# Wider slots for the side stages of a hybrid decoder step, and the weight sums issued by GpSimd

## The chip, the cores and the metric

One NeuronCore of a Trainium2 chip runs the whole program as one launch. The metric is device time in microseconds from the start to the end of an execution, and less is better. PE is TensorE, DVE is VectorE, ACT is ScalarE, POOL is GpSimd and SP is the sync engine, which here only issues DMAs.

## What is computed

One layer of a decoder with two branches, for a prompt of 2048 tokens and for 8 samples of 8 tokens each. Cut to what matters:

```python
xn = _rmsnorm(x, g_pre)
u = xn @ w_in                                    # 2112 tokens x 1024 -> 10256 columns
z = (glr @ w_gla_lr + b_gla_lr)                  # low-rank decay, from 16 columns of u
o_a, s_new = _gla(q, k, v, log_sigmoid(z) / 16, s0)      # gated linear recurrence, in chunks
y_a = (_rmsnorm(o_a) * silu(gg)) @ w_gla_branch
for (win, dil) in ((128, 1), (512, 4), (2048, 16)):      # dilated windows
    prompt: banded attention;  samples: attention over the cached rows and the 8 new ones
y_b = (softmax-weighted sum of the windows * silu(dg)) @ w_dil_branch
merged = sigmoid(ga) * y_a + sigmoid(gb) * y_b
h = x + _rmsnorm(merged @ w_out, g_post)
h = h + (pe @ w_ple_proj) * sigmoid(h @ w_ple_gate)
```

The outputs are h, the recurrence's states, and the windows' caches of keys and values.

## The kernel before

**The frame.** The product x @ w_in fills most of the run. Its 10240 wide columns are 20 column tiles of 512, and the prompt is taken in two phases of 1024 tokens, so there are 40 column tiles in time, each with two halves. A half takes seven products of a seven-product scheme for 2x2 blocks (forms P1, P6, P2, P7, P4, P5, P3 in this order) in place of eight, and each product is three fp16 matmuls (high part by high, low by high, high by low). A column tile has 336 such matmuls (L849, L851); the samples' 48 (L860) come with those of phase 0.

**Slots.** Every engine's program is one loop over 740 numbered slots, 17 for a column tile of phase 0 (8 and 9 for its halves) and 20 for one of phase 1. In each slot an engine issues its part of the product first and then what the side stages have in that slot. The slot's length in time is what PE needs for its matmuls of that slot, and the engines meet through semaphores alone. An engine that is late in a slot makes later ones late in turn.

**The weights of the next column tile.** SP loads 512 columns of w_in into two tiles `raw` (L695). The seven forms need four sums of their quarters, made in place: P7, P6, P4, P5 (`sum`, L714, L718, L722, L725). ACT then casts each form to its high part (`cut_hi`, L703) and DVE makes the low part (`cut_lo`, L707). This is timed by tables in slots from the middle of the column tile before: the high parts at 4 (P1), 5 (P2), 6 (P7), 7 (P6), 9 (P4), 10 (P5) and 11 (P3), the low part one slot later. Before the change DVE makes the sum P7 at 2, and each other sum right behind the low part that sets its quarter free: P6 behind P1, P4 behind P2, P5 behind P7. PE takes P1 at 9 (phase 0), P6 some 1.1 slots later, and so on.

**The side stages that the change touches.**

- Tokens (`Inputs`): the second 1024 prompt tokens are loaded, normed, summed and split (L442, L551), turned by a DMA transpose (L570) and stored in four pairs, the first at slot 16 and each 11 slots after the last.
- Slices (`Cutter`): 30 slices of the later weights (mixer weights) are loaded, cast by ACT (`cut_hi`, L2257), subtracted by DVE (`cut_lo`, L2263) and both parts stored by SP (L2244, L2245), from slot 95, one every 4 slots. ACT's cast waits until both stores of the slice before have landed.
- Recurrence (`Gla`, phase 0): eight steps from slot 72, one every 6 slots. `SampleGla` follows at slot 130.
- Samples (`Samples`): from slot 236, one sample every 15 slots; u is the slot within one. Caches of keys and values are loaded (ACT and POOL issue them), DVE makes row sums in slots u = 1, 3, 5, 7 (L2164, L2168) from rows that POOL loads two steps ahead (L1963), and PE turns those sums at the end of u = 8 (L2088).
- The windows of the prompt begin at slots 409, 481, 547 and the recurrence's phase 1 at 625; the mixer (L2888) follows the loop.

POOL's part before the change: norms and sums of the tokens, DMA issues of the side stages, and copies of the caches (L3070).

## Time and profile before

| what | value |
|---|---|
| median of 3 runs | 2868.7 us (2867.64 to 2869.06) |
| the profiled execution, its own time | 2873.31 us |
| its span | 2871.4 us |
| PE busy | 2671.5 us (93%) |
| DVE busy | 1767.6 us (62%) |
| ACT busy | 1035.5 us (36%) |
| POOL busy | 430.5 us (15%) |
| mean granted clock of PE | 0.971 |

The profile's page gives each engine's busy time and share of the span. A busy PE may run at either of two granted clocks, 2.4 GHz (1.0) or 1.2 GHz (0.5), so time is lost in two ways: as idle time of PE, and as busy time at the lower clock. The product's loop takes about the first 2235 us, the mixer the rest.

### The profile page before, as it was taken

What the parts mean: (1) busy time and instruction counts of PE and PEld (TensorE: products, weight loads), DVE (VectorE), ACT (ScalarE), POOL (GpSimd) and SP (SyncE); (2) the same over time, 40 slices, a digit from 0 to 9 for tenths busy, and PEclk for the clock granted to TensorE, in tenths of its full rate; (3) what the DMA queues carried; (4) which work ended last, traced back from release to release, by engine and by line L of the source; (5) the groups of instructions that cost most, each with busy time, mean ns of one, the idle gap of its engine ahead of it and who ended that gap; (6) DMA issues with size and microseconds to landing.
All of it is one profiled execution on the core that took longest, in us unless ns stands there. A gap on an engine that the chain in (4) does not pass through costs nothing. (4 is left out here: it accounts for less than half of the span.)

```text
span 2871.4 us, 54212 instructions
## 1 busy us (share of the span) xinstructions
PE 2671.5 (93%) x21916; PEld 2041.6 (71%) x21916; DVE 1767.6 (62%) x3181; ACT 1035.5 (36%) x1880; POOL 430.5 (15%) x649
## 2 busy tenths in 40 slices
PE   5788989899989999899999999999999999999998
PEld 4676878678877788788888888888887444444444
DVE  6575766665656656656677666767666455555552
ACT  4233443232222222222334445535423344444441
POOL 5132102210112122101112211011100000000000
PEclk8999999999999999999999999999999999999999
DMA  5698666888777879667757766455546976566552
GB/s 152 153 275 285 229 224 237 312 281 296 262 271 250 258 265 286 233 233 259 264 185 240 232 224 212 139 170 186 186 181 181 313 217 143 158 176 167 163 116 57
DMA packets 370058, 622.39 MB, mean 217 GB/s; under 512 B 199196, under 2 KB 204899, under 8 KB 365330
## 3 DMA queue, kind: packets, MB, share of 16 engines
q1 hardware_dynamic: 311554, 352.11, 39.2%
q0 software_dynamic: 44000, 233.26, 24.8%
q10 hardware_dynamic: 14256, 33.56, 3.3%
q8 instruction: 175, 2.87, 0.4%
q14 instruction: 73, 0.60, 0.1%
HBM read 429.15 MB, written 244.66 MB: 235 GB/s over the span
## 5 line engine op out<-in xcount | busy, mean ns | idle before, releaser
L851 PE MATMUL out<-w_hi,x_hi 128*128 128x256 f16 x3136 | 872.0, 278 | 64.0 <-DVE w_lo L707 24.7
L851 PE MATMUL out<-w_lo,x_hi 128*128 128x256 f16 x3136 | 871.8, 278 | 0.0
L851 PE MATMUL out<-w_hi,x_lo 128*128 128x256 f16 x3136 | 871.1, 278 | 0.0
L773 DVE SCALAR_TENSOR_TENSOR stage<-out,stage 128x512 f32<-128x512 f32 (+1 forms) x567 | 378.7, 680 | 362.4 <-PE out L851 257.9
L851 PEld LDWEIGHTS out<-w_hi,x_hi 128*128 128x128 f16 x3136 | 313.1, 100 | 119.1 <-DVE w_lo L707 27.4
L849 PE MATMUL out<-x_hi,w_hi 128*128 128x256 f16 x1344 | 369.3, 275 | 26.4 <-DVE w_lo L707 20.0
L849 PE MATMUL out<-x_hi,w_lo 128*128 128x256 f16 x1344 | 369.2, 275 | 0.0
L849 PE MATMUL out<-x_lo,w_hi 128*128 128x256 f16 x1344 | 369.1, 275 | 0.0
L703 ACT ACTIVATE w_hi<-raw 128x1024 f16<-128x1024 f32 x280 | 290.6, 1050 | 196.4 <-DVE raw L718 47.8
L707 DVE SCALAR_TENSOR_TENSOR w_lo<-raw,w_hi 128x1024 f16<-128x1024 f32 x280 | 343.9, 1232 | 7.6 <-ACT w_hi L703 7.5
L851 PEld LDWEIGHTS out<-w_hi,x_lo 128*128 128x128 f16 x3136 | 312.8, 100 | 42.8 <-issue 1.3
L851 PEld LDWEIGHTS out<-w_lo,x_hi 128*128 128x128 f16 x3136 | 312.7, 100 | 42.3 <-issue 1.1
L849 PEld LDWEIGHTS out<-x_hi,w_hi 128*128 128x128 f16 x1344 | 132.5, 99 | 47.6 <-DVE w_lo L707 22.2
L761 ACT ACTIVATE stage<-out 128x512 f32<-128x512 f32 (+1 forms) x81 | 47.7, 589 | 291.8 <-PE out L851 205.9
L849 PEld LDWEIGHTS out<-x_lo,w_hi 128*128 128x128 f16 x1344 | 132.6, 99 | 16.3
L1856 DVE CUSTOM_DVE_ANT_0 score<-out,mask 128x128 f32<-128x128 f32 (+1 forms) x192 | 69.8, 363 | 120.7 <-PE out L1802 110.2
L849 PEld LDWEIGHTS out<-x_hi,w_lo 128*128 128x128 f16 x1344 | 132.5, 99 | 16.0
L1841 ACT ACTIVATE prob<-score,result 128x128 f32<-128x128 f32 (+1 forms) x192 | 87.4, 455 | 103.5 <-DVE result L1859 103.0
L1831 ACT ACTIVATE query<-qT 128x128 f32<-128x128 f32 x128 | 54.8, 428 | 184.9 <-PE out L1791 184.9
L2888 PE MATMUL out<-mix_w_hi,mix_zTh 128*128 128x512 f16 (+1 forms) x408 | 118.8, 379 | 0.8 <-DMA mix_zTl<-mix_z_rowl 0.8
L2888 PE MATMUL out<-mix_w_lo,mix_zTh 128*128 128x512 f16 (+1 forms) x408 | 118.8, 379 | 0.0
L2888 PE MATMUL out<-mix_w_hi,mix_zTl 128*128 128x512 f16 (+1 forms) x408 | 118.8, 379 | 0.0
(354 smaller groups left out, 4279.3 us busy)
## 6 DMA issues: line engine op xcount, KB each, us to landing
raw<-in_w_in SPq DMA_DIRECT2D x80, 1024.0 KB, 8.9
out<-in_cache_kv_w POOLq DMA_DIRECT2D x64, 1020.0 KB, 9.0
U<-stage SPq DMA_DIRECT2D x224, 256.0 KB, 5.8
UT<-stage SPq DMA_DIRECT2D x96, 256.0 KB, 6.9
sw_kc<-in_cache_kv_w ACTq DMA_DIRECT2D x24, 1024.0 KB, 11.0
sw_vc<-in_cache_kv_w POOLq DMA_DIRECT2D x24, 1024.0 KB, 9.6
sw_rows<-U POOLq DMA_DIRECT2D x32, 512.0 KB, 7.6
out<-in_cache_kv_w POOLq DMA_DIRECT2D x16, 1008.0 KB, 7.5
```

What stands on the lines that cost most here:

```text
L703: act.activation(self.w[0][f][:, :, :], self.sources[f], ACT.Copy, scale=W_SCALE).then_inc(self.hi_ready, 1)
L707: dve.scalar_tensor_tensor(out=self.w[1][f][:, :, :], in0=self.sources[f], scalar=W_SCALE, in1=self.w[0][f][:, :, :], op0=ALU.mult, op1=AL ...
L761: act.activation(self.spot(D, 1, 0, us), self.shaped(D, self.product(D, P1, us), us), ACT.Copy, scale=1.0 / W_SCALE).then_inc(self.act_kep ...
L773: return dve.scalar_tensor_tensor(out=out, in0=self.shaped(D, self.product(D, f, us), us), scalar=1.0 / W_SCALE, in1=other, op0=ALU.mult, ...
L849: return pe.matmul(out.rearrange("p (a t) -> p a t", t=P), w[:, k, d * P:(d + 1) * P], x[:, 2 * u:2 * u + 2, f * HALF_K + k, :], start=sta ...
L851: return pe.matmul(out, x[:, 2 * d + u, f * HALF_K + k, :], w[:, k, :], start=start, stop=stop)
L1831: act.activation(self.query[n % 2][:, :], self.queries(h, b, dil), ACT.Copy)
L1841: act.activation(self.prob[n % 2][:, a:, :], self.score[n % 2][:, a:, :], ACT.Exp, scale=SCALE, bias=result[:, b, HD:HD + 1], accum_out=re ...
L1856: dve.tensor_tensor_reduce(self.score[n % 2][:, a:, :], self.SCORE[:, a * P:2 * P].rearrange("p (a j) -> p a j", j=P), self.mask[:, a:, :] ...
L2888: made = pe.matmul(made, x, w, start=(k == 0 and i == 0), stop=(k == last and i == 2))
```

## The change

It moves six tables and two kinds of work, and what is computed stays the same.

- The four sums of a column tile's weights are issued on POOL (in slots 1, 5, 7 and 8 counted from the middle of the column tile before). Those of the first column tile stay on DVE.
- Tokens: pairs begin at slot 18 and every 15 slots, and their loads are at slots 7, 8, 13 and 27, as soon as buffers are free, in place of 4 slots ahead of each pair.
- Recurrence, phase 0: from slot 84 every 8 slots; `SampleGla` at 163.
- Slices: from slot 100 every 5 slots; the high part is stored one slot after its cast and the low part one slot after that, each with its own semaphore, so that ACT waits for the high part's store alone and DVE for the low part's.
- Samples: from slot 264 every 17 slots.
- Some semaphores are reused (`left`, `later`), which makes room for the new ones.

```diff
-SUM_AT = 2
+SUM_AT = {P7: 1, P6: 5, P4: 7, P5: 8}
...
-GLA_SLOTS, GLA_PERIODS = (GLA_TILES * TILE_PARTS[0] + 4, 625), (6, 7)
-GLA_SAMPLE_SLOT = 130
-SAMPLE_SLOT, SAMPLE_PERIOD = 236, 15
+GLA_SLOTS, GLA_PERIODS = (84, 625), (8, 7)
+GLA_SAMPLE_SLOT = 163
+SAMPLE_SLOT, SAMPLE_PERIOD = 264, 17
...
-CUT_SLOT, CUT_PERIOD = 95, 4
+CUT_SLOT = 100
+CUT_TIMES = [5 * i for i in range(30)]
...
-    FIRST_SLOT, EVERY = 16, 11
+    FIRST_SLOT, EVERY = 18, 15
+    LOAD_SLOTS = (7, 8, 13, 27)
...
-            if slot == self.base(k) - 4:
+            if slot == self.LOAD_SLOTS[k - self.SAMPLE - 1]:
...
                     self.cut_lo(dve, H, f)
-                    if f in NEXT_SUM:
-                        self.sum(dve, H, NEXT_SUM[f])
-            if at == SUM_AT:
-                self.sum(dve, H, P7)
...
+    def pool(self, pool, q):
+        for H, _, at in self.coming(q):
+            for f in (P7, P6, P4, P5):
+                if at == SUM_AT[f]:
+                    self.sum(pool, H, f)
...
+        i = self.at(r - 1)
+        if i is not None:
+            sp.wait_ge(self.hi_cut, i + 1)
+            sp.dma_start(self.cut_hi[:, i, :], self.hi[:, :]).then_inc(self.hi_stored, 16)
         i = self.at(r - 2)
         if i is not None:
             sp.wait_ge(self.lo_cut, i + 1)
-            sp.dma_start(self.cut_hi[:, i, :], self.hi[:, :]).then_inc(self.stored, 16)
-            sp.dma_start(self.cut_lo[:, i, :], self.lo[:, :]).then_inc(self.stored, 16)
+            sp.dma_start(self.cut_lo[:, i, :], self.lo[:, :]).then_inc(self.lo_stored, 16)
...
-            wait(act, self.stored, 32 * i)
+            wait(act, self.hi_stored, 16 * i)
+            wait(act, self.lo_cut, i)
...
             dve.wait_ge(self.hi_cut, i + 1)
+            wait(dve, self.lo_stored, 16 * i)
...
                 G, d, c = place(q)
+                projection.pool(pool, q)
                 inputs.pool(pool, q)
```

On DVE, in the fourth sample (u = 4 to 7), where the low parts of P1, P2, P7 and P6 of the next column tile stand among the sample's row sums. Before the change (L707 is a low part, L718, L722 and L725 the sums P6, P4 and P5, L2164 and L2168 the row sums, L773 takes a product over):

```order
L707 SCALAR_TENSOR_TENSOR w_lo<-raw,w_hi 128x1024
L718 TENSOR_TENSOR raw<-raw 128x4x256
L773 SCALAR_TENSOR_TENSOR stage<-out,stage 128x2x256
L707 SCALAR_TENSOR_TENSOR w_lo<-raw,w_hi 128x1024
L722 TENSOR_TENSOR raw<-raw 128x4x256
L2164 TENSOR_TENSOR sw_rows<-sw_kc,sw_rows 128x1024
L2168 TENSOR_REDUCE sw_sT<-sw_rows 128x2x4
L773 SCALAR_TENSOR_TENSOR stage<-out,stage 128x2x256 x2
L707 SCALAR_TENSOR_TENSOR w_lo<-raw,w_hi 128x1024
L725 TENSOR_TENSOR raw<-raw 128x4x256
L773 SCALAR_TENSOR_TENSOR stage<-out,stage 128x2x256
L707 SCALAR_TENSOR_TENSOR w_lo<-raw,w_hi 128x1024
```

In the changed kernel the same place of DVE (its lines stand a few further down: L709 is the low part, L775 the product taken over, L2171 and L2175 the row sums) reads:

```order
L709 SCALAR_TENSOR_TENSOR w_lo<-raw,w_hi 128x1024
L775 SCALAR_TENSOR_TENSOR stage<-out,stage 128x2x256
L709 SCALAR_TENSOR_TENSOR w_lo<-raw,w_hi 128x1024
L2171 TENSOR_TENSOR sw_rows<-sw_kc,sw_rows 128x1024
L2175 TENSOR_REDUCE sw_sT<-sw_rows 128x2x4
L775 SCALAR_TENSOR_TENSOR stage<-out,stage 128x2x256 x2
L709 SCALAR_TENSOR_TENSOR w_lo<-raw,w_hi 128x1024
L775 SCALAR_TENSOR_TENSOR stage<-out,stage 128x2x256
L709 SCALAR_TENSOR_TENSOR w_lo<-raw,w_hi 128x1024
L2171 TENSOR_TENSOR sw_rows<-sw_kc,sw_rows 128x1024
```

The three sums are gone from among the low parts, and the rest stands in the same order.

On POOL, one whole sample of phase 0 in the changed kernel (L716, L720, L724 and L727 are the sums P7, P6, P4 and P5, L1970 the load of rows, L1955, L1976 and L1996 loads of the queries, keys and values):

```order
L716 TENSOR_TENSOR raw<-raw 128x4x256
L1970 DMA sw_rows<-U 128x2x512
L1955 DMA sw_new_k<-U 8x512
L1955 DMA sw_new_v<-U 8x512
L1955 DMA sw_q<-U 8x512
L720 TENSOR_TENSOR raw<-raw 128x4x256
L1970 DMA sw_rows<-U 128x2x512
L1976 DMA sw_new_k<-U 8x512 x3
L724 TENSOR_TENSOR raw<-raw 128x4x256
L1970 DMA sw_rows<-U 128x2x512
L727 TENSOR_TENSOR raw<-raw 128x4x256
L1970 DMA sw_rows<-U 128x2x512
```

Before, POOL had the loads alone here; now three of a sample's four loads of rows stand right behind a sum.

On SP, two slices late in the slices' stage (CUT_HI and CUT_LO are the stores of the two parts, `cut_raw` the load of a later slice, U and UT the product's results). Before the change:

```order
L2244 DMA CUT_HI<-cut_hi 128x1024
L2245 DMA CUT_LO<-cut_lo 128x1024
L2240 DMA cut_raw<-in_w_out 128x1024
L904 DMA U<-stage 128x512 x4
L2244 DMA CUT_HI<-cut_hi 128x1024
L2245 DMA CUT_LO<-cut_lo 128x1024
```

In the changed kernel:

```order
L2251 DMA CUT_HI<-cut_hi 128x1024
L908 DMA UT<-stage 128x512
L2255 DMA CUT_LO<-cut_lo 128x1024
L908 DMA UT<-stage 128x512
L2247 DMA cut_raw<-in_w_out 128x1024
L2251 DMA CUT_HI<-cut_hi 128x1024
```

The store of the high part has left the store of the low part and goes a slot earlier.

## Rows read from the trace of the kernel before

**Rows 1.** The page: span and busy time of PE and PEld, DVE, ACT, POOL.

```profile
span 2871.4 us, 54212 instructions
PE 2671.5 (93%) x21916; PEld 2041.6 (71%) x21916; DVE 1767.6 (62%) x3181; ACT 1035.5 (36%) x1880; POOL 430.5 (15%) x649
```

**Rows 2.** Stretches: length, busy (instructions) of PE, PEld, DVE, ACT, POOL, clock, DMA, GB/s.

```profile
110.00:330.00 220.00, 190.73 (x1738) 160.80 (x1737) 149.65 (x174) 73.97 (x98) 54.76 (x56) 0.94 0.80 247
330.00:586.00 256.00, 232.38 (x2052) 192.75 (x2050) 162.36 (x251) 103.72 (x143) 48.42 (x77) 0.95 0.74 257
586.00:765.00 179.00, 165.96 (x1545) 144.57 (x1544) 108.08 (x119) 49.86 (x56) 8.16 (x18) 0.96 0.81 282
765.00:1212.00 447.00, 409.65 (x4785) 352.61 (x4784) 277.92 (x387) 99.35 (x143) 99.97 (x171) 0.96 0.79 263
1212.00:1909.00 697.00, 680.99 (x5844) 600.29 (x5843) 473.95 (x1290) 272.80 (x763) 101.92 (x148) 1.00 0.64 215
1909.00:2235.00 326.00, 305.33 (x2539) 257.98 (x2538) 214.60 (x337) 128.00 (x180) 24.45 (x34) 0.97 0.57 191
```

**Rows 3.** The stretch right behind a long gap of PE, same columns.

```profile
172.00:176.50 4.50, 4.50 (x23) 3.19 (x22) 0.86 (x1) 0.00 (x0) 0.00 (x0) 0.50 1.59 201
```

**Rows 4.** Timeline, PE: start, us, engine, line, instruction [idle before, what ended it].

```profile
171.78 0.40 PE L849 MATMUL out<-x_hi,w_hi 128*128 128x256 f16 x1 [8.76 <-DVE w_lo L707]
223.54 0.39 PE L851 MATMUL out<-w_hi,x_hi 128*128 128x256 f16 x1 [8.30 <-DVE w_lo L707]
```

**Rows 5.** Timeline: DVE at a late load, and PE behind two of them.

```profile
259.54 1.23 DVE L714 TENSOR_TENSOR raw<-raw 128x1024 f32<-128x1024 f32 x1 [12.06 <-DMA raw<-in_w_in]
...
261.42 0.28 PE L851 MATMUL out<-w_hi,x_hi 128*128 128x256 f16 x1 [3.97 <-DVE stage L773]
...
805.61 0.40 PE L851 MATMUL out<-w_hi,x_hi 128*128 128x256 f16 x1 [5.50 <-DVE stage L773]
```

**Rows 6.** Slices: ACT's idle time before L2257 (us, times), the stores' landing, timeline.

```profile
  DMA CUT_LO<-cut_lo: 155.8, 23
...
DMA to landing us min/median/max: 2.3/6.1/14.1
...
420.90 1.15 ACT L2257 ACTIVATE cut_hi<-cut_raw,cut_gains 128x1024 f16<-128x1024 f32 x1 [12.01 <-DMA CUT_LO<-cut_lo]
...
422.68 0.37 PE L1236 MATMUL out<-prompt_lowrank,prompt_decay_w 51*128 51x128 f16 x2 [4.38 <-ACT prompt_k_endT L1284]
...
535.88 0.79 PE L1547 MATMUL out<-sample_v,sample_att 128*128 128x256 f32 x1 [4.28 <-ACT sample_o L1588]
```

**Rows 7.** Timeline, PE: the longest gap in the recurrence of phase 0.

```profile
393.50 0.77 PE L1261 MATMUL out<-prompt_v,prompt_k_endT 128*128 128x256 f32 x1 [4.81 <-DVE prompt_att L1330]
```

**Rows 8.** The fourth sample: DVE's first and last row of 15, PE; PE's waits there.

```profile
975.33 0.69 DVE L773 SCALAR_TENSOR_TENSOR stage<-out,stage 128x512 f32<-128x512 f32 x1 [0.42 <-PE out L851]
...
990.29 1.22 DVE L2168 TENSOR_REDUCE sw_sT<-sw_rows 128x8 f32<-128x1024 f32 x1
...
991.57 0.47 PE L2088 MATMUL out<-identity,sw_sT 128*128 128x128 f32 x1 [6.12 <-DVE sw_sT L2168]
...
PE out L2088 <- DVE sw_sT L2168: 25.6, 6, 7.2
```

**Rows 9.** Lines: ns min/median/max of DVE's sum, low part and POOL's token sum; one collision.

```profile
L714 DVE TENSOR_TENSOR raw<-raw x40: 1212/1216/1812, 13.4 to 2168.3; 128x1024 f32<-128x1024 f32 x40
...
L707 DVE SCALAR_TENSOR_TENSOR w_lo<-raw,w_hi x280: 1203/1215/2279, 15.1 to 2188.2; 128x1024 f16<-128x1024 f32 x140
...
L456 POOL TENSOR_TENSOR sums<-x x7: 1268/1278/2177, 10.4 to 224.8; 128x512 f32<-128x512 f32 x7
...
14.21 2.12 POOL L461 TENSOR_TENSOR sums<-x,sums 128x512 f32<-128x512 f32 x1
...
15.14 2.28 DVE L707 SCALAR_TENSOR_TENSOR w_lo<-raw,w_hi 128x1024 f16<-128x1024 f32 x1
```

**Rows 10.** The rows' load L1963: us from issue to landing.

```profile
DMA to landing us min/median/max: 5.3/7.6/17.3
```

More of the change, by code:

```diff
@@ L1060, in queue, with left @@
                 sp.dma_start(self.L[:, SEQ:TOKENS], self.last[:, :]).then_inc(self.stored, 16)
+    def left(self):
+        return [(self.cut, 3 * PHASES), (self.made, PHASES), (self.kept, 2 * self.CHUNKS + 3)]
     def done(self, eng, phase):
@@ L1917, in __init__ @@
         self.rows_loaded = [one(f"rows_loaded{s}") for s in range(self.RING)]
-        self.k_loaded = [one(f"k_loaded{p}") for p in range(len(self.K_PIECES) + 1)]
+        self.k_loaded = [later(f"sw_k_loaded{p}") for p in range(len(self.K_PIECES))] + [Later(one("new_k_loaded"), 0)]
         self.v_loaded = one("v_loaded")
@@ L1973, in load_k @@
             after(q, self.k_turned, c * N_TURNED)
-            self.load_new(q, c, self.new_k, U_DK, self.k_loaded[p])
+            self.load_new(q, c, self.new_k, U_DK, self.k_loaded[p].sem)
             return
@@ L1982, in load_k @@
             after(q, self.k_turned, (c - 1) * N_TURNED + blocks.stop)
-        q.dma_start(self.kc[:, blocks, :], src).then_inc(self.k_loaded[p], 16)
+        q.dma_start(self.kc[:, blocks, :], src).then_inc(self.k_loaded[p].sem, 16)
     def load_v(self, q, c):
@@ L2058, in tensor @@
             p = self.turned_piece(n)
-            pe.wait_ge(self.k_loaded[p], 16 * (c + 1) * (1 if n < N_CACHE else GROUPS))
+            after(pe, self.k_loaded[p], 16 * (c + 1) * (1 if n < N_CACHE else GROUPS))
             after(pe, self.k_kept, c * N_TURNED + i - 1)
@@ L2161, in vector @@
             p = max(p for p, (g, low, _) in enumerate(self.K_PIECES) if CACHE_BLOCKS.index((g, low)) <= first)
-            dve.wait_ge(self.k_loaded[p], 16 * (c + 1))
+            after(dve, self.k_loaded[p], 16 * (c + 1))
             dve.wait_ge(self.rows_loaded[x % self.RING], 16 * (x // self.RING + 1))
@@ L2224, in __init__ @@
         self.lo_cut = one("lo_cut")
-        self.stored = one("stored")
+        self.hi_stored = one("hi_stored")
+        self.lo_stored = one("lo_stored")
     def at(self, r):
-        i, u = divmod(r, CUT_PERIOD)
-        return i if u == 0 and 0 <= i < len(self.slices) else None
+        return CUT_TIMES.index(r) if r in CUT_TIMES else None
     def gain(self, i):
@@ L2235, in queue @@
     def queue(self, sp, r):
-        i = self.at(r + CUT_PERIOD + 1)
+        i = self.at(r + 5)
         if i is not None:
@@ L2243, in queue @@
             sp.wait_ge(self.lo_cut, i + 1)
-            sp.dma_start(self.cut_hi[:, i, :], self.hi[:, :]).then_inc(self.stored, 16)
-            sp.dma_start(self.cut_lo[:, i, :], self.lo[:, :]).then_inc(self.stored, 16)
+            sp.dma_start(self.cut_lo[:, i, :], self.lo[:, :]).then_inc(self.lo_stored, 16)
     def done(self, eng):
-        wait(eng, self.stored, 32 * len(self.slices))
+        wait(eng, self.hi_stored, 16 * len(self.slices))
+        wait(eng, self.lo_stored, 16 * len(self.slices))
     def scalar(self, act, r):
@@ L2961, in run_layer @@
                 windows = Windows((core.bind(part)[0], sem), side, U, UT, a["window_mask"], identity, OG, kv_prompt[0])
-        left = iter(inputs.left() + sample_gla.left() + prompt_gla.left() + windows.left())
+        left = iter(inputs.left() + sample_gla.left() + prompt_gla.left() + windows.left() + lowrank.left())
         def later(name):
@@ L3032, in _ @@
                     lowrank.queue(sp, phase, q - LOWRANK_SLOTS[phase])
-                if q == CUT_SLOT - CUT_PERIOD - 4:
+                if q == CUT_SLOT - 8:
                     lowrank.done(sp, 0)
```

## The prediction, made before the changed kernel ran

> **What bounds the kernel now.** I read the page first: PE is busy 2671.5 of 2871.4 us [rows 1], so at most 200 us of idle time, and what PE does at the lower clock, can be won. The view of stretches says where that lies. From 110 to 1212 us (phase 0, with tokens, recurrence, slices and samples beside the product) PE lacks 29.3, 23.6, 13.0 and 37.4 us (length less busy time) and its clock stands at 0.94 to 0.96; from 1212 to 1909 us (windows) it lacks 16.0 us at a clock of 1.00, and from 1909 to 2235 us 20.7 us at 0.97 [rows 2]. A gap costs more than its length: right behind the one that ends at 171.78 us the granted clock is 0.50, which is 1.2 GHz, for 4.5 us [rows 3]. PE was busy all that time and did half the work, so 2.25 us are lost besides the gap; I charge that to each gap over 3.5 us. The change touches phase 0 above all, so I then went through PE's gaps there and asked of each what ended it.
>
> **Tokens (110 to 330 us).** Two gaps of 8.76 and 8.30 us end on the low part of a weight [rows 4]. Counting off 336 product matmuls a column tile, both stand 24 matmuls into one, at P6, in slots 35 and 52. DVE was behind: the low parts of the seven forms must be made in slots 13 to 20 of a column tile's 17 (up to P6 in 13 to 16), and pairs 2 and 4, with bases 27 and 49, put their splitting in slots 31 and 32 and their scaling in 49 and 50, into just these. A third gap, 3.97 us, has another cause: DVE itself had stood 12.06 us at the sum P7, whose load was late, and took no products over meanwhile [rows 5]. With bases 18, 33, 48 and 63 the splitting of the second pair is at 37 and 38 and out of the way, loads are early, and a late load now stops POOL and not DVE. Removed: 8.76 + 8.30 + 3.97 + 3 x 2.25 = 27.8 us. But pairs 3 and 4 now scale in slots 48, 49, 63 and 64, beside the low parts, with POOL's token sums (four of 1.28 us each [rows 9]) among the weight sums. I put back 10 us for that. **Net -18 us** (-28 to -5).
>
> **Slices (345 to 765 us).** ACT waits 155.8 us, in 23 of 30 slices, for the store of the low part; a store takes 6.1 us to land in the median, at most 14.1 [rows 6]. Before, two slots (some 5 to 6 us) lie between the issue of the stores and the next cast. While ACT stands it makes no high parts and takes nothing else over: the wait of 12.01 us that ends at 420.90 us delays `prompt_k_endT`, and PE stands 4.38 us for it; the gap of 4.28 us at 535.88 us ends on ACT too [rows 6]. After the change four slots lie between each store and its waiter, 10 to 13 us, over the median and a little under the worst. From 586 to 765 us little else runs than slices, so all its loss counts: 13.0 us idle, and of the clock's deficit of 0.04 x 179 = 7.2 us some six tenths, 4.3 us (part of the lower clock falls into gaps and costs nothing). That makes 17.3 us, and 2 x (4.3 + 2.25) = 13.1 us with the two gaps ahead of it: 30 us. Since P6's chain stays tight (below), I take three quarters. **-23 us** (-30 to -10).
>
> **Recurrence (300 to 500 us).** What else the stretch 330 to 586 us lost is 23.6 + 0.6 x 12.8 - 13.1 = 18 us; its longest gap is 4.81 us behind DVE's `prompt_att` [rows 7]. Eight slots a step in place of six thin DVE's work per slot by a quarter, but the masked copy and the product behind it stay one slot apart. I take half. **-9 us** (-16 to 0).
>
> **Weight sums from DVE to POOL.** DVE loses 39 x 4 instructions of 1.22 us [rows 9], 190 us in all, and none of that is a gain by itself, as PE is not waiting for DVE's mean. What counts is DVE in the four slots in which it makes P1, P2, P7 and P6. The price on POOL: its tensor_tensor on 128x512 takes 1.28 us alone, so 2.5 us for a sum of 128x1024 (an estimate from that row). And the two engines block each other: L707, whose inputs both lie in SBUF, took 2.28 us in place of 1.22 beside a POOL sum, which itself took 2.12 in place of 1.27 [rows 9]. So a sum of 2.5 us on POOL may hold DVE's next low part for up to 2.3 us, against 1.22 us saved.
>
> The Trainium skill says the same as a rule (SBUF — State Buffer, section SBUF: two separate sides): the port pair that DVE and GpSimd share is an exclusive lock held for a whole instruction, and a DVE instruction with two SBUF inputs takes part in it. By that rule alone the offload is worth about nothing wherever DVE is behind; had the two not blocked each other, each column tile would have 4.9 us less of DVE. The collision in rows 9 agrees.
>
> The samples show what that does. In the fourth one DVE works without a pause from 975.33 to 991.51 us, 16.2 us for 15 instructions, and PE has stood 6.12 us [rows 8]. Without three sums of 1.22 us that is 12.5 us and a gap of 2.5 us; with POOL holding DVE by 1 to 1.8 us at each of three low parts it is 6 us again. This sample began 9 slots into a column tile. A period of 17 and a start at 264 = 15 x 17 + 9 give all five samples that lie in phase 0 this place, while the eight of now lose 25.6 us, in six gaps [rows 8], and 6 x 2.25 us of clock, 39 us in all. Five at 6.1 + 2.25 are 42 us: no change; at 2.5 + 2.25, -15; and if the rows that POOL loads behind a sum come late (7.6 us to landing, up to 17.3 [rows 10], used three slots later), up to +15. The 5.50 us at 805.61 us, again behind a late load of weights [rows 5], go, as the caches' first loads start six slots ahead of the weights and no longer just with them: -7. **Samples together -7 us** (-22 to +8).
>
> In the windows PE lacks only 16.0 of 697 us [rows 2]. ACT must wait longer for a sum of 2.5 us, and DVE is held now and then: **+5 us** (0 to +20) for 13 column tiles. In the recurrence's phase 1, whose slots don't move, both effects meet: **0** (-8 to +8).
>
> **Costed at nothing.** SP issues as many DMAs as before; POOL's waits for stores and for DVE's results name work of two slots earlier, so they don't hold a sum that stands behind them. POOL's busy time grows by 39 x 4 x 2.5 = 390 us to some 820 of 2871: not a bound.
>
> **The sum.** -18 - 23 - 9 - 7 + 5 + 0 = -52 us. From the profiled execution's 2873.3 us that gives 2821; the median of the runs lies 4.6 us below that execution, so **2817 us**. Its own range is 2798 to 2842, from the terms' ranges taken together and not all at one end.
>
> **The rivals.**
>
> *DVE is freed for real.* If POOL's sums mostly fall where DVE takes products over (from PSUM, which no row shows blocked), the samples win 15 more, the put-back at the tokens is 4 and not 10, and phase 1 gains its 8: 2817 - 29 = 2788. For it: DVE waits for PE often enough outside phase 0's crowded slots. Against: the sums stand right behind low parts, where DVE goes on to the next one. Chance 0.19.
>
> *Gaps move and don't go.* P6's chain (low part of P1, sum, cast, low part) is no shorter, so the slots in which slices and tokens were late turn out late by P6 again: tokens and slices bring a third. -14 - 5 - 7 + 5 = -21: about 2848. Chance 0.14 for that; 0.06 that it lies within 0.2% of now (2863 to 2874).
>
> *POOL makes P6 late, and the kernel slower.* The place is P6 in each of the 19 column tiles from 110 to 1156 us. On POOL the sum waits for a low part (1.2 us), takes 2.5 in place of 1.22, the low part of P6 waits behind the next sum (up to 2.5), and three sums (3.7) no longer stand ahead of it: +1.3 us; with three DMA issues between the sums, +3. PE takes P6 only 5 slots behind the low part of P1, some 13 to 16 us. At 2.5 us and 2.25 of clock each, 19 x 4.75 = 90 us against the 52 won: 2817 + 90 = 2907. It decides from 2.7 us a tile with the clock. Against it: the low parts saved from ahead of P6 nearly pay for it. Chance 0.13. It is also what the rule of the Trainium skill (same page and section) would make of it, if POOL got the lock first each time.
>
> That the change doesn't do what it says is out: on DVE the sums are gone and on POOL they stand.
>
> **How the numbers follow.** The forecast itself has 0.48 of the chance. All cases but the last two are faster: 0.48 + 0.19 + 0.14 = 0.81; same 0.06; slower 0.13. A measurement can tell about 0.2%, 6 us, from no change. The range takes the forecast, most of the better case, and the lesser gain up to no change: 2785 to 2872.
>
> **What would show it.** Tokens: no gaps of over 4 us in the first 330 us behind the first column tile. Slices: ACT's wait for CUT_LO gone, for CUT_HI under 30 us. Sums: POOL's rows at 2.5 us alone and 3.5 or more beside DVE, L709's longest at 3 us or more. Samples: five gaps at the turning of the row sums, each 2 to 7 us; if they are gone, the lock bites less than I think. I am wrong if PE shows a gap at P6 in most column tiles (slower), or if PE's idle time in phase 0 behind the first column tile, 103 us now (110 to 1212 us), stays over 75 us (tokens and slices were not the cause).

## The result: 0.6% slower, and the profile after

The changed kernel takes 2885.9 us in the median (2883.2 to 2889.3) against 2868.9 us before: a ratio of 1.0058 (95% interval 1.0039 to 1.0078). The forecast was 2817 us, with a range of 2785 to 2872; the time lies outside it and on the other side of no change. The profiled execution took 2889.3 us, its span is 2887.4.

The page after, span and busy time, answers to [rows 1]:

```profile
span 2887.4 us, 54244 instructions
PE 2666.2 (92%) x21916; PEld 2041.8 (71%) x21916; DVE 1734.1 (60%) x3025; ACT 1036.0 (36%) x1880; POOL 824.9 (29%) x805
```

POOL is at 825 us, as forecast (some 820). DVE lost 156 sums of 1.22 us, 190 us, and is only 33.5 us less busy. Where most of that went stands in the costliest groups of after (busy us, mean ns | idle before, and what ended it):

```profile
L709 DVE SCALAR_TENSOR_TENSOR w_lo<-raw,w_hi 128x1024 f16<-128x1024 f32 x280 | 455.5, 1632 | 14.5 <-ACT w_hi L705 14.3
...
L720 POOL TENSOR_TENSOR raw<-raw 128x1024 f32<-128x1024 f32 x39 | 99.8, 2560 | 442.2 <-DVE w_lo L709 442.2
```

The low parts (L709, L707 before) are the same 280 instructions. Their mean was 1232 ns before and is 1632 ns now: 112 us more of DVE. The next largest are the recurrence's `prompt_to_end` (8.0 us more) and the samples' `sw_rows` (5.7). And POOL stands 442 us ahead of P6's sum (L720), waiting for a low part of DVE: whatever POOL has queued behind that sum waits as well.

By stretches (columns as in [rows 2]); the bounds are the ends of the same column tiles, so that the same products stand in a row of before and of after; matmuls of the side stages have moved between rows (1738 and 1627 PE instructions in the first). First after, then, of before, the stretch with the samples, which [rows 2] cuts elsewhere:

```profile
107.50:311.30 203.80, 174.66 (x1627) 147.33 (x1625) 131.43 (x118) 58.77 (x75) 96.92 (x70) 0.96 0.87 238
311.30:552.10 240.80, 224.59 (x1982) 193.52 (x1982) 162.94 (x230) 109.53 (x147) 63.41 (x57) 0.96 0.68 239
552.10:754.00 201.90, 185.45 (x1723) 154.18 (x1721) 118.91 (x140) 56.88 (x72) 76.35 (x76) 0.95 0.81 282
754.00:1299.80 545.80, 489.76 (x5459) 421.41 (x5457) 315.19 (x405) 122.05 (x167) 203.78 (x221) 0.95 0.77 257
1299.80:1922.50 622.70, 604.49 (x5174) 536.30 (x5172) 407.60 (x1196) 255.63 (x744) 196.66 (x178) 0.99 0.64 213
1922.50:2251.50 329.00, 302.94 (x2539) 256.99 (x2538) 217.75 (x313) 128.34 (x181) 89.28 (x61) 0.97 0.57 190
```

```profile
764.50:1286.10 521.60, 483.41 (x5458) 418.25 (x5456) 321.90 (x437) 116.09 (x161) 103.96 (x179) 0.96 0.77 258
```

Length less PE's busy time, before and after: tokens 29.3 and 29.1 us; recurrence 23.6 and 16.2; slices 13.0 and 16.5; samples 38.2 and 56.0. Together 104 and 118 us. At 754 us the changed kernel is still 10 us ahead (764.5 before), although part of the recurrence's work has moved into the slices' column tiles. The samples' column tiles take that away and 14 us more (1299.8 against 1286.1); the windows are even, and the recurrence's phase 1 loses 3 us.

What PE waits for after (us in all, times, longest):

```profile
PE out L2095 <- DVE sw_sT L2175: 49.3, 8, 6.9
PE out L855 <- DVE w_lo L709: 34.5, 10, 6.7
PE out L853 <- DVE w_lo L709: 15.6, 4, 5.8
```

The turning of a sample's row sums (L2095; L2088 before) cost 25.6 us in six gaps [rows 8] and costs 49.3 in eight. The two gaps of 8.76 and 8.30 us at P6 [rows 4] are gone, but fourteen others stand at P6 with 50 us (18 with 44.7 us before, those two among them). Three more stalls are new or larger (PE's timeline): in the recurrence, at P6, and in the windows.

```profile
310.73 0.39 PE L1243 MATMUL out<-prompt_lowrank,prompt_decay_w 51*128 51x128 f16 x2 [6.09 <-DMA prompt_decay_w<-WS]
...
496.47 0.39 PE L855 MATMUL out<-w_hi,x_hi 128*128 128x256 f16 x1 [6.65 <-DVE w_lo L709]
...
1538.51 0.48 PE L1798 MATMUL out<-identity,k 128*128 128x128 f32 x1 [8.74 <-ACT kT L1839]
```

The first of them comes from a load that POOL issued late, behind the sum P7 (L716) whose own weights came late:

```profile
298.52 2.35 POOL L716 TENSOR_TENSOR raw<-raw 128x1024 f32<-128x1024 f32 x1 [26.14 <-DMA raw<-in_w_in]
...
302.38 0.54 POOL L1204 DMA_DIRECT2D prompt_decay_w<-WS  x1
```

"A late load now stops POOL and not DVE", which the prediction counted as a gain, has this price: what POOL issues next stops too.

ACT's wait for the slices' stores, 155.8 us in 23 [rows 6], is now for the high part alone:

```profile
ACT cut_hi L2269 <- DMA CUT_HI<-cut_hi: 62.2, 7, 16.3
```

### The profile page after: what moved, and what is told of

Read it like the earlier page. It is cut to its first block and busy times, and to the rows that moved or that the text cites. A ratio compares the mean times of both kernels' runs of the same rounds, so it can differ in the third digit from the quotient of the medians.

```text
span 2887.4 us, 54244 instructions
## 1 busy us (share of the span) xinstructions
PE 2666.2 (92%) x21916; PEld 2041.8 (71%) x21916; DVE 1734.1 (60%) x3025; ACT 1036.0 (36%) x1880; POOL 824.9 (29%) x805
## 5 line engine op out<-in xcount | busy, mean ns | idle before, releaser
L775 DVE SCALAR_TENSOR_TENSOR stage<-out,stage 128x512 f32<-128x512 f32 (+1 forms) x567 | 378.4, 680 | 451.6 <-PE out L855 317.8
L709 DVE SCALAR_TENSOR_TENSOR w_lo<-raw,w_hi 128x1024 f16<-128x1024 f32 x280 | 455.5, 1632 | 14.5 <-ACT w_hi L705 14.3
L720 POOL TENSOR_TENSOR raw<-raw 128x1024 f32<-128x1024 f32 x39 | 99.8, 2560 | 442.2 <-DVE w_lo L709 442.2
L716 POOL TENSOR_TENSOR raw<-raw 128x1024 f32<-128x1024 f32 x39 | 96.0, 2461 | 241.3 <-DMA raw<-in_w_in 241.0
L853 PEld LDWEIGHTS out<-x_lo,w_hi 128*128 128x128 f16 x1344 | 134.0, 100 | 17.8 <-issue 0.2
## 6 DMA issues: line engine op xcount, KB each, us to landing
U<-stage SPq DMA_DIRECT2D x224, 256.0 KB, 4.4
UT<-stage SPq DMA_DIRECT2D x96, 256.0 KB, 5.7
sw_vc<-in_cache_kv_w POOLq DMA_DIRECT2D x24, 1024.0 KB, 10.6
```

The lines of the kernel that those rows point to most:

```text
L709: dve.scalar_tensor_tensor(out=self.w[1][f][:, :, :], in0=self.sources[f], scalar=W_SCALE, in1=self.w[0][f][:, :, :], op0=ALU.mult, op1=AL ...
L716: eng.tensor_tensor(self.sources[P7], self.sources[P7], self.sources[P3], ALU.subtract).then_inc(self.sum_ready, 1)
L720: eng.tensor_tensor(self.sources[P6], self.sources[P1], self.sources[P7], ALU.subtract).then_inc(self.sum_ready, 1)
L775: return dve.scalar_tensor_tensor(out=out, in0=self.shaped(D, self.product(D, f, us), us), scalar=1.0 / W_SCALE, in1=other, op0=ALU.mult, ...
L853: return pe.matmul(out.rearrange("p (a t) -> p a t", t=P), w[:, k, d * P:(d + 1) * P], x[:, 2 * u:2 * u + 2, f * HALF_K + k, :], start=sta ...
```

## Experiments

Medians are compared with that of the kernel before in the same comparison (2868.6 to 2871.4 us).

**1. The sums, with the new spacing and with the old.** In one kernel the sums go back to VectorE; in the other they alone are moved.

```diff
--- after
+++ sums_on_vector
-SUM_AT = {P7: 1, P6: 5, P4: 7, P5: 8}
+SUM_AT = 2
...
                     self.cut_lo(dve, H, f)
+                    if f in NEXT_SUM:
+                        self.sum(dve, H, NEXT_SUM[f])
+            if at == SUM_AT:
+                self.sum(dve, H, P7)
...
-                projection.pool(pool, q)
```

> The changed kernel with its weight sums put back on VectorE, in their old places; all wider spacing stays. Theory A (the sums on GpSimd cost what the spacing wins: VectorE's low parts are held, P6 comes late, loads stand behind sums in POOL's queue): the fourteen gaps at P6 (49 us together) and the stall of 6.09 us at 310.73 us go or fall to half, the eight gaps at the turning of the samples' sums fall from 5.9 to some 2.5 us, so 2800 to 2835 us. Rival B (the samples' new spacing costs it, whoever makes the sums): 2870 to 2890 us, with the eight gaps still at 5 to 7 us. The prediction's own terms without its term for the sums would give about 2820 us.

> The kernel before with only the weight sums moved to GpSimd. Theory A: slower than before by 30 to 60 us, 2900 to 2930 us, with gaps at P6 in many column tiles. Rival B (sums harmless, the spacing costs): within 6 us of before, 2863 to 2875 us. The prediction priced this part at 0 to +20 us.

Measured: 2872.7 us with all the spacing and the sums on VectorE (1.0022 of before, 1.0002 to 1.0041); 2874.6 us with the sums moved alone (1.0022, 1.0005 to 1.0038). Both times lie in rival B's range and outside theory A's. But the sums do cost, 13 us with the new spacing and 6 with the old, and **all the spacing together gains nothing without them**. With the sums back, the turnings still cost 45.8 us in eight gaps. Neither theory holds alone.

**2. The samples' place.** Moved alone in the kernel before; then at another place in the changed kernel, and there with the sums on VectorE too (both_vector_273).

```diff
--- before
+++ samples_alone
-SAMPLE_SLOT, SAMPLE_PERIOD = 236, 15
+SAMPLE_SLOT, SAMPLE_PERIOD = 264, 17
--- after
+++ samples_273
-SAMPLE_SLOT, SAMPLE_PERIOD = 264, 17
+SAMPLE_SLOT, SAMPLE_PERIOD = 273, 16
```

> The kernel before with the samples alone moved, to slot 264 and every 17. The prediction's term is -7 us (-22 to +8): 2847 to 2877, most likely 2862 us. Theory D: five turnings at P6's slots with 6 us each and three in the short slots of phase 1, where the rows land late, in place of 25.6 us in all: 2880 to 2896 us, with eight gaps at the turning of 45 us or more together.

> The changed kernel with the samples at slot 273 and every 16 slots in place of 264 and 17; sums stay on GpSimd. The turning of the row sums then stands outside the slots in which VectorE makes P1, P2, P7 and P6, in all samples but one or two. Theory A: the gaps at the turning shrink only where no sum of POOL holds VectorE or a load; 2865 to 2880 us. Rival B: the eight gaps fall from 49 us to under 20, with their clock 2840 to 2855 us.

> Both of the above: all spacing of the changed kernel, sums on VectorE, samples at slot 273 and every 16. Theory A: a few us below the kernel with the sums back alone, 2790 to 2825 us. Rival B: 2835 to 2855 us, the same as with the samples moved alone.

Measured: 2890.4 us alone (1.0066, 1.0039 to 1.0093), **19 us slower**, as theory D said; 2886.2 us with 273 and the sums on GpSimd, no change; 2858.6 us with 273 and the sums on VectorE (0.9976, 0.9949 to 1.0002; ten runs from 2848 to 2886), 14 us below the kernel with 264. Neither theory's range held at 273. So the place costs, but at 273 four samples turn in phase 1, and their gaps stay (39.2 and 32.3 us in all eight; of the 32.3, with the sums on VectorE, the four in phase 0 have 0.2 to 2.5 us each and the four in phase 1 3.7 to 9.8). PE's waits at the turning, samples_alone:

```profile
PE out L2088 <- DVE sw_sT L2168: 45.2, 8, 6.7
```

The eight gaps have two causes. Five samples start nine slots into a column tile, and their last step meets the low parts of P2, P7 and P6. In after DVE has no pause there, and PE waits 5.9 us for the last row below (timeline, DVE):

```profile
946.90 1.22 DVE L709 SCALAR_TENSOR_TENSOR w_lo<-raw,w_hi 128x1024 f16<-128x1024 f32 x1
948.03 0.68 DVE L775 SCALAR_TENSOR_TENSOR stage<-out,stage 128x512 f32<-128x512 f32 x1
948.63 2.99 DVE L709 SCALAR_TENSOR_TENSOR w_lo<-raw,w_hi 128x1024 f16<-128x1024 f32 x1
951.54 1.21 DVE L2171 TENSOR_TENSOR sw_rows<-sw_kc,sw_rows 128x1024 f32<-128x1024 f32 x1
952.79 1.22 DVE L2175 TENSOR_REDUCE sw_sT<-sw_rows 128x8 f32<-128x1024 f32 x1
```

Here 2.99 in place of 1.22 us is a sum of POOL (948.21 to 950.54 us). With the sums on VectorE the gap is 6.11 us: what the offload saves, the wait gives back. The other three samples lie in phase 1, where a column tile is cut into 20 slots and not 17, and a slot without other work is 37.3 / 20 = 1.9 us (two column tiles of phase 1 took 74.5 us before). DVE there waits for the rows themselves (after, DVE and then POOL):

```profile
1225.95 1.23 DVE L2171 TENSOR_TENSOR sw_rows<-sw_kc,sw_rows 128x1024 f32<-128x1024 f32 x1 [6.17 <-DMA sw_rows<-U]
...
1216.35 0.75 POOL L1970 DMA_DIRECT2D sw_rows<-U  x1 [6.01 <-DVE sw_sT L2175]
```

The load can be issued only when the step two before it has freed its buffer, and lands some 9 us later, in slots of 1.9 us. Without any sum on POOL it is the same (4.57 us for these rows). In the kernel before, one sample of eight turned in phase 1, which begins at 1156 us, and had the longest gap (before, PE):

```profile
1187.53 0.47 PE L2088 MATMUL out<-identity,sw_sT 128*128 128x128 f32 x1 [7.25 <-DVE sw_sT L2168]
```

**3. The tokens and POOL's copies.** In the kernel with all the spacing and the sums on VectorE, SP's transposition of the second pair took 32.96 us; the eight transpositions of these pairs before took 4 to 10. POOL issues four of the copies that shift the caches within 6 us, the last two just then (timeline, SP and POOL); copies_apart moves these two from slot 44 to slot 231:

```profile
175.71 1.11 POOL L3081 DMA_DIRECT2D out<-in_cache_kv_w  x2
180.27 32.96 SPq L572 DMA_TRANSPOSE row1h<-row0h  x1
180.72 0.96 POOL L3081 DMA_DIRECT2D out<-in_cache_kv_w  x2 [3.90 <-PE out L851]
```

```diff
--- sums_on_vector
+++ copies_apart
-SHIFT_PAIRS = (range(3, 27), range(42, 62))
+SHIFT_PAIRS = ((3, 4, *range(6, 28)), range(42, 62))
```

> The kernel with all the new spacing and the sums on VectorE, but without the two cache copies that POOL issues in slot 44; they are issued at slot 231. Theory C: with the new spacing SP's transposition of the second pair of token tiles begins beside these copies and takes 33 to 41 us where it took 4 to 8, and everything behind it on SP comes late; apart, it takes under 11 us and the stall of 11 us in the tokens goes: 2855 to 2862 us, against 2872.7 with the copies there. Rival: the transposition is slow for another reason, or its delay is hidden: 2867 to 2876 us.

Measured: 2859.8 us (0.9959, 0.9946 to 0.9972), 13 us less. The transposition now:

```profile
179.89 6.90 SPq L572 DMA_TRANSPOSE row1h<-row0h  x1
```

In that kernel column tiles 1 to 4 lose 17.8 us of PE, against 33.4 with the copies there and 29.3 before. The fair comparison is recurrence_alone (below), where the recurrence has left these column tiles too and the tokens are as before: 26.2 us. So the wider tokens do gain, some 8 us, once nothing stands in SP's way. In after the second transposition of this pair took 22.4 us and the first landed 29 us after its issue.

**4. Slices and recurrence**, each alone on the kernel before; the slices keep their period of four.

```diff
--- before
+++ stores_apart
+        i = self.at(r - 1)
+        if i is not None:
+            sp.wait_ge(self.hi_cut, i + 1)
+            sp.dma_start(self.cut_hi[:, i, :], self.hi[:, :]).then_inc(self.hi_stored, 16)
         i = self.at(r - 2)
         if i is not None:
             sp.wait_ge(self.lo_cut, i + 1)
-            sp.dma_start(self.cut_hi[:, i, :], self.hi[:, :]).then_inc(self.stored, 16)
-            sp.dma_start(self.cut_lo[:, i, :], self.lo[:, :]).then_inc(self.stored, 16)
+            sp.dma_start(self.cut_lo[:, i, :], self.lo[:, :]).then_inc(self.lo_stored, 16)
...
-            wait(act, self.stored, 32 * i)
+            wait(act, self.hi_stored, 16 * i)
+            wait(act, self.lo_cut, i)
...
+            wait(dve, self.lo_stored, 16 * i)
--- before
+++ recurrence_alone
-GLA_SLOTS, GLA_PERIODS = (GLA_TILES * TILE_PARTS[0] + 4, 625), (6, 7)
-GLA_SAMPLE_SLOT = 130
+GLA_SLOTS, GLA_PERIODS = (84, 625), (8, 7)
+GLA_SAMPLE_SLOT = 163
```

> The kernel before with one part alone: the stores of a slice's high and low part are issued and waited for apart; period and all other places as before. The prediction's term for slices was -23 us with the period of five. If that is right, three slots in place of two between a store and its waiter bring most of it: 2848 to 2858 us, with ACT's wait for stores under 80 us. Rival (what the slices lose, VectorE's chain to P6 loses anyway): 2864 to 2872 us.

> The kernel before with the recurrence alone moved: every 8 slots from 84, samples' recurrence from 163. The prediction's term is -9 us (0 to -16): 2856 to 2866 us. Theory E: no gain, 2868 to 2878 us, with gaps at P6 in the recurrence's column tiles and the slices, now beside the samples' recurrence, no better.

Measured: stores apart 2852.5 us (0.9941, 0.9924 to 0.9958), **17 us faster**, though ACT still waits 106.8 us; recurrence alone 2871.4 us (1.0012, 0.9998 to 1.0026), no gain. Eight slots a step put two steps into 16 of a column tile's 17 slots, so every second one meets P6 again, with gaps of 5.06 and 5.42 us at slots 120 and 137 (4.42 and 0.47 us before). More is lost behind it: column tiles 9 to 12 lack 24.7 us of PE, against 13.0 before. `SampleGla` now begins in them, beside the slices; a slice's store, which there took 20.2 us to land, holds up ACT, and ACT holds up PE (recurrence_alone, ACT and then PE):

```profile
595.84 1.06 ACT L2257 ACTIVATE cut_hi<-cut_raw 128x1024 f16<-128x1024 f32 x1 [21.96 <-DMA CUT_LO<-cut_lo]
...
597.44 0.39 PE L851 MATMUL out<-w_hi,x_hi 128*128 128x256 f16 x1 [9.00 <-ACT stage L761]
```

The stores apart gain mostly in the recurrence's column tiles: the stretches of 256.0 and 179.0 us [rows 2] take 239.1 and 175.0.

**5. What the parts are worth together.** Tokens wide with the copies apart, stores apart with the old period, sums on VectorE; the samples at 236 or 227; then the recurrence every 6 slots again. Beside these, stores_samples is stores_apart with the samples at 227 and every 15, and nothing else moved.

```diff
--- copies_apart
+++ spaced_236
-CUT_SLOT = 100
-CUT_TIMES = [5 * i for i in range(30)]
+CUT_SLOT = 95
+CUT_TIMES = [4 * i for i in range(30)]
-SAMPLE_SLOT, SAMPLE_PERIOD = 264, 17
+SAMPLE_SLOT, SAMPLE_PERIOD = 236, 15
--- spaced_236
+++ spaced_227
-SAMPLE_SLOT, SAMPLE_PERIOD = 236, 15
+SAMPLE_SLOT, SAMPLE_PERIOD = 227, 15
--- spaced_227
+++ spaced_recur6
-GLA_SLOTS, GLA_PERIODS = (84, 625), (8, 7)
-GLA_SAMPLE_SLOT = 163
+GLA_SLOTS, GLA_PERIODS = (84, 625), (6, 7)
+GLA_SAMPLE_SLOT = 142
```

> Tokens and recurrence as in the changed kernel, with copies and transposition apart; slices with stores apart but at the old start and period (95, 4); samples at their old places (236, 15); sums on VectorE. Theory D (the samples' new place is what costs the spacing its gain, since three of them now turn in phase 1, whose slots of 1.9 us are too short for a load of rows of 6 to 16 us): 2830 to 2850 us. Rival (the samples' place matters little): 2855 to 2865 us, as with the copies apart.

> The same with the samples at slot 227 and every 15, so that seven of the eight turn in phase 0 and the last at its very end. Theory D: 6 to 14 us less than with 236, 2820 to 2840 us, and no gap over 4 us at a turning. Rival: the same time as with 236 within 5 us.

> The kernel before with two parts: a slice's stores apart (old period), and the samples at slot 227 and every 15. Tokens, recurrence and sums as before. Theory D: the samples give here too what they gave between 236 and 227 with all spaced, 12 us, or a little more: 2834 to 2842 us against 2852.5 with the stores alone. Rival (the gain of 227 hangs on the spacing of the rest): 2848 to 2855 us.

> The kernel with tokens spaced, copies and transposition apart, slices 95 and 4, samples 227 and 15, sums on VectorE, and now the recurrence every 6 slots from 84 (samples' recurrence at 142) in place of every 8 from 84 (163). Theory E: eight slots a step gain nothing, since two steps in 16 of a column tile's 17 slots fall on P6 in nearly the same place tile after tile (gaps of 5.06 and 5.43 us at slots 120 and 137): 2825 to 2838 us against 2843.3. Rival, the prediction's (six slots a step are too thin for VectorE): 2848 to 2856 us.

Measured: 2854.8, 2843.3, 2833.5 and **2824.5 us** (the last 0.9849 of before, 0.9825 to 0.9872). With 236 I was wrong: no gain over the stores alone, since the later recurrence took back what the tokens gave (column tiles 1 to 4, which it has left in part, take 193 us in place of 219 in stores_apart; 9 to 12, into which its end has moved, 203 in place of 175). From 236 to 227 the samples gain 12 us, on the old spacing 19 (2852.5 to 2833.5). The turnings are the lesser part of that (27.4 to 24.8 us and 29.2 to 24.1, with gaps over 4 us left where I expected none); a gap behind late weights in column tile 13, of 6.04 and 6.84 us, goes as well. Six slots a step, with `SampleGla` at 142, gain 19 us over eight: column tiles 5 to 8 lack 17.2 us of PE in both kernels, 9 to 12 lack 6.4 in place of 19.8.

**6. Why the sums cost.** On stores_samples (2833.5 us) all sums go to GpSimd as in the change (stores_samples_pool); then they stand behind the loads of the same slot; then only P4 and P5 go, in the place that the change gives them.

```diff
--- stores_samples_pool
+++ loads_first
-                projection.pool(pool, q)
                 inputs.pool(pool, q)
...
                 side_queue(pool, q)
+                projection.pool(pool, q)
--- stores_samples
+++ sums_half
+POOL_AT = {P4: 7, P5: 8}
...
-                    if f in NEXT_SUM:
+                    if f == P1:
                         self.sum(dve, H, NEXT_SUM[f])
...
+    def pool(self, pool, q):
+        for H, _, at in self.coming(q):
+            for f in (P4, P5):
+                if at == POOL_AT[f]:
+                    self.sum(pool, H, f)
```

> The same with the weight sums on GpSimd: the price of the sums where little else is late. Theory A: 10 to 20 us more than with the sums on VectorE, 2846 to 2860 us, with L709-like low parts of over 1.5 us in the mean and new gaps at P6 and behind POOL's loads. Rival (the sums cost only where they meet the samples' bad place): within 4 us of the same kernel with sums on VectorE.

> The kernel with a slice's stores apart, samples at 227 and sums on GpSimd (2859.7 us; 2833.5 with sums on VectorE), with POOL's sums issued behind the loads and stores of the same slot, not ahead of them. Theory F (the sums cost because they wait for VectorE's low parts and hold the loads queued behind them): the stall of 8.64 us in the windows goes, 2840 to 2850 us. Rival G (the price is the lock and the longer way to P6): 2855 to 2866 us, the stall in the windows gone or not, the gaps at P6 as they were.

> The same kernel with P7 and P6 summed on VectorE and only P4 and P5 on GpSimd. Rival G, way to P6: the gaps at P6 are those of the kernel with all sums on VectorE, and so is the time within 6 us, 2830 to 2840 us. Rival G, lock alone: about half of the price of 26 us stays, 2843 to 2850 us. Theory F, queue: sums of P4 and P5 wait for VectorE too, and hold the loads: 2843 us or more, with the stall in the windows there.

Measured: 2859.7, 2854.9 and 2845.7 us. The sums cost **26 us** where less else is late, more than I expected. Against stores_samples, the stretches of tokens, slices, samples and the recurrence's phase 1 are 8, 4, 8 and 10 us longer, that of the windows 3 us shorter. The queue (theory F) is a part: with the sums in front, POOL waits 15 us for a low part and issues the windows' loads behind it. (In the order that POOL has for one sample of the changed kernel, all four loads of rows stand right behind a sum, and not three.) In after, timeline of POOL ahead of the stall at 1538.51 us:

```profile
1516.71 2.35 POOL L720 TENSOR_TENSOR raw<-raw 128x1024 f32<-128x1024 f32 x1 [15.31 <-DVE w_lo L709]
1519.02 1.58 POOL L1729 DMA_DIRECT2D k<-U  x2
```

Behind the loads the stall is gone and the windows' stretch is 10.6 us shorter (618.9 to 608.3), but the samples lose 7 of it, the tokens 5, and the time falls by 5 only. Half of the sums cost half, 12 us, and the gaps at P6 stay although P7 and P6 are summed on VectorE, while the stall in the windows that theory F wanted is absent. All gaps at P6 are 44.9 us in stores_samples, 59.3 with all sums on POOL, 60.6 with the loads first and 60.6 with half. The same P6 in stores_samples, with all sums on POOL, and with half (timeline, PE):

```profile
576.02 0.28 PE L851 MATMUL out<-w_hi,x_hi 128*128 128x256 f16 x1 [2.22 <-DVE w_lo L707]
```

```profile
584.68 0.39 PE L853 MATMUL out<-w_hi,x_hi 128*128 128x256 f16 x1 [4.08 <-DVE w_lo L707]
```

```profile
584.14 0.28 PE L856 MATMUL out<-w_hi,x_hi 128*128 128x256 f16 x1 [3.66 <-DVE w_lo L708]
```

So it is not P6's longer way, and the queue is a lesser part. That the rest is the lock between the two engines is argued from the durations; no run takes the lock alone away. In after 115 low parts meet a sum of POOL (of weights or tokens) and take 2.2 us in the mean, the other 165 take 1.22. The Trainium skill (SBUF — State Buffer, section SBUF: two separate sides) makes the shared port pair an exclusive lock and counts in a VectorE instruction with two SBUF inputs. The trace agrees: L709 and L2171 are held (five of L2171 meet a sum and take 2.4 us in the mean, the others 1.21), while L775, with one input in PSUM, took 0.68 us in the mean in its 155 cases beside a sum (128x512), 0.69 without.

**7. The sums in the windows alone.** In the windows the sums behind the loads had given the shortest stretch; so they are moved there alone, on the fastest kernel.

```diff
--- spaced_recur6
+++ windows_on_pool
+POOL_TILES, POOL_AT = range(23, 34), {P7: 1, P6: 5, P4: 7, P5: 8}
...
-                    if f in NEXT_SUM:
+                    if f in NEXT_SUM and H not in POOL_TILES:
...
+    def pool(self, pool, q):
+        for H, _, at in self.coming(q):
+            for f in (P7, P6, P4, P5):
+                if at == POOL_AT[f] and H in POOL_TILES:
+                    self.sum(pool, H, f)
...
                 side_queue(pool, q)
+                projection.pool(pool, q)
```

> The fastest kernel so far (spaced_recur6, 2824.5 us) with the weight sums of column tiles 23 to 33 alone, the windows, on GpSimd, and there behind the loads of the same slot. Theory H (the sums on GpSimd cost where VectorE is crowded and gain in the windows, where it is not: the stretch of column tiles 23 to 33 took 608.3 us with POOL's sums behind the loads, 621.9 with sums on VectorE): 2808 to 2816 us. Rival G (the lock costs everywhere, and the shorter stretch came from elsewhere): 2822 to 2832 us.

Measured: **2810.8 us** (0.9806, 0.9783 to 0.9829), 13.6 us less. The stretch of the windows without and with it (columns as in [rows 2]):

```profile
1239.00:1861.10 622.10, 607.38 (x5175) 534.84 (x5173) 430.06 (x1240) 256.01 (x745) 98.06 (x140) 1.00 0.63 214
```

```profile
1238.00:1847.10 609.10, 601.06 (x5174) 534.58 (x5173) 410.73 (x1197) 257.74 (x746) 195.87 (x182) 1.00 0.65 219
```

PE lacks 8.0 us in place of 14.7 and is itself busy for 6.3 us less with the same products; why its busy time falls no run here tells. With the sums on POOL the low parts are held there as elsewhere, 31 of 77 meeting a sum (DVE by lines in these stretches, without and then with):

```profile
L709 DVE SCALAR_TENSOR_TENSOR w_lo<-raw,w_hi 128x1024 f16<-128x1024 f32 x77 | 93.4, 1215 | 0.0
```

```profile
L710 DVE SCALAR_TENSOR_TENSOR w_lo<-raw,w_hi 128x1024 f16<-128x1024 f32 x77 | 123.5, 1605 | 0.0
```

So it is not because the low parts are spared that the sums pay there. In the windows some six tenths of VectorE's instruction time go to instructions that read PSUM, in the samples' column tiles under four tenths (spaced_recur6); that this is the reason is a guess that no run tests.

## Why the prediction was wrong, term by term

The parts measured alone make up the result: stores -17, recurrence +2, samples +19, sums +6, tokens +7 (column tiles 1 to 4 with the sums on VectorE lose 33.4 us of PE, 26.2 in recurrence_alone; read from stretches, not run alone): +17 us, and +17 measured. That it meets so well is luck in part: the sums cost 6, 13 or 26 us by what else has moved, and in spaced_236 stores, recurrence and tokens (-8 with the copies apart) should bring -23 and brought -15. The slices' period of five and their later end were not run alone.

- **Samples, -7: the step that failed worst.** Alone they cost 19 us. "Five samples in phase 0" at 6.1 us each were right (5.90 to 6.45 in after). I costed the three in phase 1 at nothing, and they cost 5.5 to 6.9. The row for it stood in [rows 8]: the longest wait, 7.2 us, was that of the one sample that turned in phase 1, and I did not ask where it stood (I called all of 110 to 1212 us phase 0, which ends at 1156). The 5.50 us behind late weights, which made the -7, did go. Also, the five were priced against the eight of before, which left three of eight out of the sum.
- **Tokens, -18.** What I said of DVE's crowded slots was right: the two long gaps went, and pairs 3 and 4 do scale beside low parts (7.50 us at slot 69, 5.31 at 86 in spaced_227), 12.8 us in these two gaps, 17 with the clock at my own price, where I had put back 10. Under "Costed at nothing" I counted SP's DMAs and not what they now run beside. With the sums on VectorE the transposition beside the copies took the gain away, and apart the tokens gain some 8 us. In after the same transposition took 22.4 us; the copies were not moved alone there.
- **Slices, -23.** That ACT's wait for the stores costs PE was right: stores apart alone give -17, inside the range. But most of it comes in the recurrence's column tiles (17 us shorter) and not in 586 to 765 us (4 us shorter), to which I gave more than half of the term. ACT's wait for CUT_LO is gone, but for CUT_HI 62 us stay where I wanted under 30. In after the slices' column tiles lack 16.5 us, 8.7 with the sums on VectorE: gaps at P6 there are 10.9 us, and a product of `SampleGla` waits 5.54 us for DVE at 602.60.
- **Recurrence, -9.** Alone it is +2. The argument went over DVE's mean work per slot. It left out which slot meets P6 (a period of 8 in tiles of 17 meets it every second time) and, the larger part, that eight slots a step push `SampleGla` in among the slices (column tiles 9 to 12: 24.7 us in place of 13.0).
- **Weight sums, with windows +5 and phase 1 0.** The lock was foreseen, its sum not: 112 us of DVE, and 6, 13 or 26 us of time, the more the less else is late. POOL's sum took 2.35 us alone (estimate 2.5). "They don't hold a sum that stands behind them" looked at POOL's queue in one direction; the sums hold the loads (8.74 us in the windows, 6.09 at 310.73). Phase 1 takes 4 us more in after than in sums_on_vector, and 10 more in stores_samples_pool than in stores_samples. In the windows after is even, and with the loads in front and no sums elsewhere on POOL the kernel gains 13.6 us, so there the sign was wrong: the gain of the better rival, "DVE is freed for real", in one stretch, though the low parts are held there too.
- **The rivals.** "POOL makes P6 late" (0.13) comes nearest: gaps at P6 in 12 of the first 20 column tiles, of 1.9 to 6.7 us, though with 50 us in all they are hardly more than the 44.7 before. Then, too, 12 of these column tiles had one, so that a gap at P6 in most of them, my sign for this rival, could not tell. It took them together with the samples to end on that side, and no rival of mine was that. The other sign that I named, PE's idle time staying over 75 us, was met: 118 us through the samples, against 104.

## What to carry to other kernels

When work is moved to other slots, go through every engine and queue that it issues on at the new place, SP's transpositions and POOL's copies too, and through the length of a slot there; a period is judged against the period of what it must avoid, and by what it pushes into the next stage. Before sums go from VectorE to GpSimd, try it one stretch at a time, with the loads in front in GpSimd's queue: here it paid in the windows and cost beside the tokens, the slices, the samples and the recurrence's phase 1. A wait that occurs once and is the longest is the first to look up.

## What was unexpected of the hardware

A DMA transposition that takes SP 4 to 10 us took 33 us (41 in both_vector_273) when four DRAM copies were issued within 6 us around it, and the two copies issued with it landed 23 and 35 us later, where 6 to 11 is usual. And a low part can be held for longer than one sum: up to 5.07 us in after. One that began during POOL's DMA issues waited for the sum that started 0.8 us later (timeline):

```profile
303.26 4.24 DVE L709 SCALAR_TENSOR_TENSOR w_lo<-raw,w_hi 128x1024 f16<-128x1024 f32 x1
...
303.48 0.55 POOL L1206 DMA_DIRECT2D prompt_causal_sb<-in_causal_prompt  x1
304.04 2.36 POOL L720 TENSOR_TENSOR raw<-raw 128x1024 f32<-128x1024 f32 x1
```

The 24 low parts that met a DMA issue of POOL and no sum took 1.22 us, so the issue by itself does not hold them; what let the later sum go first is not settled.
